# Two transformer blocks on one core: where the norm factor of the up projection is applied, and where expert weights land

## What is computed

```
h = rms_norm(x, g_pre_ffn)
u = causal_depthwise_conv(h @ w_up, conv_w, conv_b)      # 1024 -> 5632, 3 taps
gate, val = split(u)
f = (gelu(gate) * val) @ w_down                           # 2816 -> 1024
x = x + rms_norm(f, g_post_ffn)
e = p @ w_ple                                             # embedding, 256 -> 1024
g = sigmoid(rms_norm(x, g_ple_gate) @ w_ple_gate + b_ple_gate)
x = x + rms_norm(g * e, g_post_ple)
```

## Time and profile before

| | |
|---|---|
| median of three runs | 919.2 us (918.31 to 919.8) |
| the profiled execution, its own time | 917.52 us |
| its span, first to last instruction | 915.6 us |
| granted clock of TensorE, mean | 0.924 |
| PE busy | 769.0 us (84%) |
| DVE / ACT / POOL busy | 383.0 / 328.8 / 128.0 us |
| moved by DMA | 298.48 MB, mean 326 GB/s |

### The profile page before, as it was taken

One profiled execution on the slowest core, in us unless ns is written; L12 is line 12 of the kernel. 1 busy time (PEld: TensorE's weight loads), 2 busy tenths in 40 slices (PEclk: granted clock), 3 DMA queues, 4 the chain that ended last, 5 costly groups with the idle time before them and its releaser, 6 DMA issues.

```text
span 915.6 us, 12692 instructions
## 1 busy us (share of the span) xinstructions
PE 769.0 (84%) x5298; PEld 527.4 (58%) x5298; DVE 383.0 (42%) x838; ACT 328.8 (36%) x656; POOL 128.0 (14%) x130
## 2 busy tenths in 40 slices
PE   9999999999999999999999985668675575655575
PEld 7986579999998867898785431223221222212223
DVE  5757776667779764899613110010100100101002
ACT  5756767666665467824723010001000000000012
POOL 0021042555541033103010000000000000000000
PEclk9999999999999999999999997878778887887877
DMA  9956709755069782646579999999999999999995
GB/s 356 422 193 230 318 1 374 292 185 184 2 278 394 280 337 78 263 175 229 220 306 356 428 447 420 431 434 432 437 433 422 432 437 425 436 432 428 432 421 241
DMA packets 19359, 298.48 MB, mean 326 GB/s; under 512 B 2144, under 2 KB 2528, under 8 KB 5856
## 3 DMA queue, kind: packets, MB, share of 16 engines
q1 hardware_dynamic: 19296, 297.61, 78.7%
HBM read 296.55 MB, written 1.05 MB: 325 GB/s over the span
## 4 chain that ended last, share of the span: by engine, by line
PE 56%; DMA 30%; DVE 9%; ACT 3%; issue 1%; SPq 0%; DVEq 0%; ACTq 0%
PE ps L114 56%; DMA ring<-in_exps 30%; DVE ar L140 3%; DVE fr L132 2%; ACT L120 1%; DVE ar L132 1%; DVE hT L140 0%; ACT sq L120 0%; PE ps L117 0%; ACT ar L123 0%; DVE xg L140 0%; ACT ar L120 0%; ACT yT L120 0%; DVE yT L140 0%; ACT hT L120 0%
## 5 line engine op out<-in xcount | busy, mean ns | idle before, releaser
L114 PE MATMUL ps<-fr 128*128 128x256 f32 (+2 forms) x1308 | 206.7, 314 | 1.1 <-ACT fr L120 0.4
L114 PEld LDWEIGHTS ps<-fr 128*128 128x128 f32 (+1 forms) x1308 | 182.9, 189 | 19.3 <-issue 2.1
L114 PE MATMUL ps<-ring,sq 128*32 128x512 f32 x944 | 129.7, 703 | 74.9 <-DMA ring<-in_exps 74.5
L114 PE MATMUL ps<-ring,ar 128*32 128x512 f32 (+4 forms) x792 | 97.1, 594 | 49.4 <-DMA ring<-in_exps 45.4
L114 PEld LDWEIGHTS ps<-ring,sq 128*32 128x32 f32 x944 | 31.8, 126 | 163.6 <-DMA ring<-in_exps 87.9
L132 DVE TENSOR_TENSOR fr<-ring,fr 128x512 fp32r<-128x512 f32 (+1 forms) x120 | 93.8, 808 | 40.2 <-ACT fr L123 40.1
L132 DVE TENSOR_TENSOR ar<-ar,ps 128x512 f32<-128x512 f32 x9 | 6.2, 687 | 242.3 <-PE ps L114 241.3
L114 PEld LDWEIGHTS ps<-ring,ar 128*32 128x32 f32 (+1 forms) x792 | 29.8, 125 | 101.5 <-issue 50.9
L123 ACT ACTIVATE fr<-ring 128x512 fp32r<-128x512 f32 (+1 forms) x139 | 80.1, 622 | 22.6 <-PE ps L114 20.0
L123 ACT ACTIVATE ar<-ps 128x512 f32<-128x512 f32 (+4 forms) x48 | 27.2, 571 | 153.6 <-PE ps L117 130.7
L132 DVE TENSOR_TENSOR ar<-ps,ar 128x512 f32<-128x512 f32 (+6 forms) x38 | 23.4, 632 | 120.5 <-PE ps L114 120.2
(11 more groups left out here) (193 smaller groups left out, 896.5 us busy)
## 6 DMA issues: line engine op xcount, KB each, us to landing
ring<-in_exps SPq DMA_DIRECT2D x21, 4096.0 KB, 28.4
ring<-in_exps SPq DMA_DIRECT2D x10, 6144.0 KB, 26.9
ring<-in_modw SPq DMA_DIRECT2D x12, 2048.0 KB, 13.8
ring<-in_exps SPq DMA_DIRECT2D x12, 2048.0 KB, 12.6
ring<-in_wup SPq DMA_DIRECT2D x11, 2048.0 KB, 14.0
ring<-in_wdown SPq DMA_DIRECT2D x5, 2048.0 KB, 12.7
ring<-in_exps SPq DMA_DIRECT2D x9, 1024.0 KB, 10.8
ring<-in_win SPq DMA_DIRECT2D x4, 2048.0 KB, 11.2
```

The costliest lines, as they stand in the source:

```text
L114: return Issue(self.e and self.e.matmul(o, l, r, start=start, stop=stop, skip_group_check=True))
```

## The change

Up slabs: x is rounded right after the residual add, times `g_pre_ffn` but without the norm factor. PE starts slab 0 on that; the squares, their sums, the root and the turned factor are made during slabs 0 and 1, and DVE multiplies each finished bank by the factor (`normed`, two instructions a slab, 128x512 in PSUM) ahead of `conv_base` and the taps, which move back by one to two parts. f, f_hi and f_lo move behind part 7, f_hi and f_lo into the next slab behind parts 1 and 0, and `mod_column` from part 1 to part 7. `mod_total(1)` moves ahead into the output projection; the silu of the conditioning row moves into slab 4, and the gelu table is loaded again in slab 5. Six parts of slab 0 have their rests on POOL.

Embedding: p and `w_ple` are rounded during the down stage (five roundings on ACT, five rests on POOL), and `embed` makes three products of rounded parts. The gate's first half uses banks 0 and 7, so that it no longer waits until the embedding has left its banks. In the next stage half a `mod_half` stands where idle products stood.

Routing: `token_major` writes its rows straight into the output banks and leaves them there for the sum, `over_tokens` goes; the last squares are summed by PE, not first by DVE; an expert product waits for its own x tile only.

Expert loads: piece 6 and piece 7 are loaded place by place, with waits of their own; the first half of piece 12 goes into `xT`, and the other halves of 12 to 14 follow half a slot behind.

```diff
-POOL_UP = {("lo", 0, k) for k in (0, 1, 2, 3, 5, 7)} | {("lo", j, k) for j in range(1, 11) for k in (3, 7)}
+POOL_UP = {("lo", 0, k) for k in range(6)} | {("lo", j, k) for j in range(1, 11) for k in (3, 7)}
...
+        def half_place(j, h):
+
+            if (j, h) == (12, 0):
+                return xT
+            i, o = {(12, 1): (0, 0), (13, 0): (0, 2048), (13, 1): (4, 0), (14, 0): (4, 2048), (14, 1): (1, 0)}[j, h]
+            return slot("exps", i)[:, o:o + 2048]
...
             column_sums(5, [(tile(sq, k), act_wo["osq", k // 2]) for k in range(4)]).then_inc(pe_wo, "sums", 1)
+            mod_total(1)
             out_products(range(2), 1, range(1))
...
-            pe.wait_ge(act_wo["root", 1])
-            idle_products(1, 5)
-            token_sums("mix", 2, dve_joint["mix", "mt", 1, 0])
-            idle_products(1, 5)
-            token_columns("mix", 2)
-            idle_products(2, 5)
-            pe.wait_ge(dve_joint["mix", "rrecip"])
-            turned_over(3, misc[:, 118:120]).then_inc(pe_joint, "mix", "over")
-            mod_total(1, act_wo["root", 1])
...
+                    if (j, k) == (0, 7):
+                        column_sums(2, [(tile(sq, i), pool_up["squares", i // 4]) for i in (0, 1, 4, 5)]).then_inc(pe_joint, "mix", "sums")
+                    if (j, k) == (1, 0):
+                        token_columns("mix", 2)
+                    if (j, k) == (1, 1):
+                        pe.wait_ge(dve_joint["mix", "rrecip"])
+                        turned_over(3, misc[:, 118:120]).then_inc(pe_joint, "mix", "over")
...
             def embed(j, n, *free):
-                pe.wait_ge(loaded("wple", 0), landed["p"]["all"], *free)
+                _, ph, pl = p_parts()
+                pe.wait_ge(pool_gate["p_lo"], *free)
                 for k in range(2):
-                    t = pe.matmul(bank(5 + j), ar[:, pT + k * S + 128 * j:pT + k * S + 128 * j + 128],
-                                  slot("wple", 0)[:, k * 1024 + 512 * n:k * 1024 + 512 * n + 512], k == 0, k == 1)
+                    _, wh, wl = ple_parts(2 * k + n)
+                    c = slice(k * S + 128 * j, k * S + 128 * j + 128)
+                    pe.matmul(bank(5 + j), ph[:, c], wh, k == 0, False)
+                    pe.matmul(bank(5 + j), ph[:, c], wl, False, False)
+                    t = pe.matmul(bank(5 + j), pl[:, c], wh, False, k == 1)
                 t.then_inc(pe_gate, "e", j, n)
...
             token_sums("ple", 2, dve_joint["ple", "x", 1])
-            idle_products(1, 5)
+            mod_quarter(11, 1, 0)
             token_columns("ple", 2)
-            mod_half(11, 1)
+            mod_quarter(11, 1, 1)
...
-                return tuple((act_exp if i in (1, 3, 7) else dve_exp)["x", 0, i] for i in (k - k % 2, k - k % 2 + 1))
+                return ((act_exp if k in (1, 3, 7) else dve_exp)["x", 0, k],)
...
-            x_squares("mix")
-            joint_row("mix", 2, 116)
-            for k in range(8):
-                act.wait_ge(dve_up["h", k])
-                act.copy(tile(fr, k, XH), tile(yT, k)).then_inc(act_up, "x_hi", k)
+
+            def up_input(k):
+                act.wait_ge(dve_joint["mix", "x", k])
+                act.copy(tile(fr, k, XH), tile(xT, k), col("g_pre_ffn", k)).then_inc(act_up, "x_hi", k)
+
+            for i in range(4):
+                up_input(2 * i)
+                if i == 3:
+                    up_rounded(0, 6)
+                up_input(2 * i + 1)
+                if i == 3:
+                    up_rounded(0, 7)
+                act.activation(sq[:, i * 512:(i + 1) * 512], xT[:, i * 512:(i + 1) * 512], ACT.Square).then_inc(act_joint, "mix", "xsq", i)
+                if i in (1, 2):
+                    up_rounded(0, 3 + i)
+            up_rounded(1, 0)
+            up_rounded(1, 1)
+            act.wait_ge(pe_joint["mix", "sums"])
+            act.copy(sd[:, 0, :], half(2, 0)).then_inc(act_joint, "mix", "sums")
+            up_rounded(1, 2)
+            act.wait_ge(pe_joint["mix", "cols"])
+            row_root(misc[:, 116:118], ps[:, 2, S:S + 2], 32 * 1024).then_inc(act_joint, "mix", "rroot")
+            act.activation(misc[:, 2:3], eps, ACT.Gelu_apprx_tanh).then_inc(act_up, "tables")
 
 
             def conv_base(j, p):
-                act.wait_ge(pe_up[j, 7], pool_up["f_lo", j - 2] if j > 1 else dve_up["x_lo", 7])
+                act.wait_ge(dve_up["normed", j, p], pool_up["f_lo", j - 2] if j > 1 else None)
                 for i in range(2):
                     f = 2 * j + i + 22 * p
                     act.activation(conv_place(j, p)[:, S * i:S * i + S], half(up_bank(j, p), i), ACT.Identity, scale=col("conv_w", 88 + f),
                                    bias=col("conv_b", f)).then_inc(act_up, "base", j, p, i)
 
             def conv_step(j, step):
-                if step == 1:
+                if step == 3:
                     conv_base(j, 0)
-                elif step == 3:
+                elif step == 4:
                     conv_base(j, 1)
                 elif step == 5:
                     act.wait_ge(dve_up["conv", j, 0])
                     act.activation(conv_place(j, 0), conv_place(j, 0), ACT.Gelu_apprx_tanh).then_inc(act_up, "gelu", j)
-                elif step == 7:
+                elif step == 9:
                     act.wait_ge(pool_up["f", j])
                     act.copy(fr[:, FH + 512 * j:FH + 512 * j + 512], conv_place(j, 0)).then_inc(act_up, "f_hi", j)
 
-            for j in range(11):
-                for k in range(8):
-                    if j or k > 3:
-                        up_rounded(j, k)
-                    if j:
+            for j in range(1, 11):
+                for k in range(3 if j == 1 else 0, 8):
+                    up_rounded(j, k)
+                    if j == 1:
+                        conv_step(0, k - 1)
+                    else:
                         conv_step(j - 1, k)
-                if j == 0:
-                    act.wait_ge(landed["crow"]["all"])
-                    act.activation(sq[:, 0:1024], sq[:, 0:1024], ACT.Silu).then_inc(act_mod, "crow")
+                        if k == 1:
+                            conv_step(j - 2, 9)
+                    if (j, k) == (4, 6):
+                        act.wait_ge(landed["crow"]["all"])
+                        act.activation(sq[:, 0:1024], crow, ACT.Silu).then_inc(act_mod, "crow")
+                    elif (j, k) == (5, 1):
+                        act.activation(misc[:, 2:3], eps, ACT.Gelu_apprx_tanh).then_inc(act_up, "again")
...
-                if i > 1 and i % 2 == 0:
-                    conv_step(10, i // 2)
-                if (f, n) == (8, 1):
+                if i == 1:
+                    conv_step(9, 9)
+                if i in (6, 8, 10, 18):
+                    conv_step(10, {6: 3, 8: 4, 10: 5, 18: 9}[i])
+                if (f, n) == (11, 1):
                     act.activation(misc[:, 2:3], eps, ACT.Sqrt).then_inc(act_down, "tables")
+                if i in (30, 33, 36, 39):
+                    w, hi, _ = ple_parts((i - 30) // 3)
+                    act.wait_ge(loaded("wple", 0))
+                    act.copy(hi, w).then_inc(act_gate, "ple", (i - 30) // 3)
+                if i == 27:
+                    p, hi, _ = p_parts()
+                    act.wait_ge(landed["p"]["all"])
+                    act.copy(hi, p).then_inc(act_gate, "p")
...
+            def input_rest(k):
+                dve.wait_ge(act_up["x_hi", k])
+                dve.scalar_tensor_tensor(tile(fr, k, XL), tile(xT, k), col("g_pre_ffn", k), tile(fr, k, XH).bitcast(F32),
+                                         ALU.mult, ALU.subtract).then_inc(dve_up, "x_lo", k)
+
+            def normed(j, p):
+
+                u = by(bank(up_bank(j, p)), S)
+                dve.wait_ge(pe_up[j, 7], dve_joint["mix", "row"])
+                dve.tensor_tensor(u, u, wide(rb[:, 1, :], 2), ALU.mult).then_inc(dve_up, "normed", j, p)
+
+            def up_rest(j, k):
+                if ("lo", j, k) not in POOL_UP:
+                    hi, lo = weight_place(8 * j + k)
+                    dve.wait_ge(act_up["hi", j, k])
+                    dve.tensor_tensor(lo, slot("wup", j)[:, 512 * k:512 * k + 512], hi.bitcast(F32), ALU.subtract).then_inc(dve_up, "lo", j, k)
+
             for k in range(9):
                 if k < 8:
-                    dve.wait_ge(pe_joint["mix", "over"])
-                    dve.scalar_tensor_tensor(tile(yT, k), tile(xT, k), col("g_pre_ffn", k), half(3, 0), ALU.mult, ALU.mult).then_inc(dve_up, "h", k)
+                    add_turned("mix", k, (6, 7, 0, 1)[k // 2], col("g_post_mix", k))
                 if k:
-                    dve.wait_ge(act_up["x_hi", k - 1])
-                    dve.tensor_tensor(tile(fr, k - 1, XL), tile(yT, k - 1), tile(fr, k - 1, XH).bitcast(F32), ALU.subtract).then_inc(
-                        dve_up, "x_lo", k - 1)
-            mod_total(1)
...
                 for k in range(8):
-                    if ("lo", j, k) not in POOL_UP:
```

(68 more changed lines are left out.)

141 lines of the change are left out of this document (78 added, 63 removed).

## The result

The changed kernel takes 923.45 us (median of six runs, 921.47 to 924.05) against 918.96 for the kernel before: a ratio on record of 1.0046 (not quite the quotient of the two medians), 95% interval 1.0036 to 1.0057, so 0.46% slower. Its profiled execution has a span of 921.5 us, 5.9 more than before. By the medians it is 4.5: the execution that was profiled before took 917.52 us, less than its median, so differences between the two profiles add up to 1.4 too much. The forecast was 921.8 and slower. One execution of the last experiment ran at a mean granted clock of 0.555 and took 1258.69 us, the other four 910.4 to 912.29; without it the median given there, 911.59, would be 911.53.

The account below looks back on a forecast made before the run. TensorE's chain was taken to bound the kernel first, the DMA engines in the experts; terms summed to +2.55 us on the profiled 917.52, giving 920.1, with the median 1.7 above at 921.8. Range 909 to 928, the forecast's own 918 to 927.

Parts of the forecast that it names:

- The start: Start of the up projection: slab 0's products begin 6.8 us sooner; `mod_total` in the output projection gives back 0.7.
- The loop of VectorE: Up slabs: f and f_lo on GpSimd exclude VectorE's rests, so its loop is 11.56 us against PE's 11.45.
- slabs without a column: Slabs 2 to 7: each costs 0 to 0.7 us, taken as 0.4 x 6 = +2.4.
- behind columns: Loops beginning with a column in slabs 8 to 10: 2.2 us over PE's, three times, +6.6; start of down +1.05.
- the silu and the table load: ACT in slabs 4 and 5: silu and second gelu load ahead of roundings cost 0 to 2 us, taken +0.7.
- slabs 0 and 1: First two up slabs: starting without a lead costs 0.5 to 3 us, taken +1.5; sums between products add +1.7.
- Rival A: Up slabs: GpSimd falls into VectorE's waits, PE stays the bound, loop terms go; sum -9.2, 910.0 us; chance 0.22.
- Rival B: Up slabs: only columns bite, 1.3 us in each of three slabs and 0.5 in down; 914.4 us; chance 0.16.
- Embedding and gate: Embedding to gate: rounded products and freed banks save 0.4 to 1.7 us, taken -1.3; the quarter `mod_half` -0.4.
- Routing: Routing to expert products: no VectorE squares, no wait for the second x tile, `over_tokens` gone; -1.2 us.
- The loads: Expert loads: 1 MiB more place in `xT` shortens the dense DMA stream, taken -2.4 us, between -3.8 and +0.6.
- Rival C: Expert loads: the extra MiB gives nothing or loses up to 0.6, the rest as forecast; about 924.5 us; chance 0.17.

Follow-up runs that it names:

- the last experiment: Changed kernel with f and f_lo on VectorE, all squares summed by TensorE and the gelu table loaded two parts later: 911.59 us, 0.9921 of the kernel before.
- short columns: Changed kernel with the four columns of slabs 7 to 10 made over 8 of their 1024 elements: 916.54 us, 0.9974 of the kernel before.
- 1.75 by the experiment: Changed kernel with a plain copy instead of the silu in slab 4 and no second gelu table load: 921.7 us, 1.0035 of the kernel before.
- the first experiment: Changed kernel with f and its rest f_lo moved from GpSimd to VectorE: 913.54 us, 0.9944 of the kernel before.
- the two experiments with f: Changed kernel with f and f_lo on VectorE, 913.54 us; changed kernel with GpSimd's f on 8 of 512 columns, 913.51 us.
- the kernel with halves in the ring: Changed kernel with the six halves of pieces 12 to 14 in ring slots as before, none in xT: 926.29 us, 1.0088 of the kernel before.

## Why the prediction was right

**The start** was right: from the first output products (106.20 before, 107.32 after) to slab 0 it is 34.63 before and 28.38 after, 6.25 less, against 6.8 - 0.7 = 6.1 forecast. The execution was already 1.1 late at the output products; over the profiles of the changed kernel and its variants, all the same up to there, they begin between 106.25 and 107.32, so that part of the difference is scatter.

**The loop of VectorE** was right in its mechanism and nearly in its size. For the terms between slab 0 and the gate I had 1.7 + 1.5 + 2.4 + 6.6 + 1.05 + 0.7 = 13.95, and 141.44 - 127.08 = 14.36 up to down, and 0.96 in down, were measured. Within it:
- slabs without a column: 11.56 was forecast for a loop with f and f_lo in it, and slabs 3, 4 and 6 have 11.6. Slab 2 lasts from 163.25 to 175.87, 12.62, and lost 12.62 - 11.52 = 1.1, so these cost 1.3 together, not 2.4. Slab 2's part went by ACT's wait for f as well, which the sum did not have.
- behind columns: slabs 7 to 10 lost 1.04 and three times 1.88, 6.7, against 7.65 with the start of down. With short columns it is 6.9 less. The upper bound in the sum, 14.6, does not come out of its own terms: 12.77 and a rest of 1.30 are 14.07. The middle of 12.77 and 14.07 is 13.42, and 13.40 was measured.
- the silu and the table load: 0.7 was taken and 13.71 - 11.52 = 2.2 measured, 1.75 by the experiment. The sum counted the silu and one table load. ACT's lines have two loads, 1.28 us each, at 193.13 and 199.82, with a silu of 1.06, and between them the wait of 2.12 for f. ACT has time for the silu and the loads alone (the first experiment), but not with that wait, and VectorE's loop had no room left to catch up with late roundings. This term was mis-sized most.
- slabs 0 and 1: from 135.70 to 163.25 it is 27.55, two slabs are 23.04, the three groups of sums 0.64 + 0.50 + 0.38 = 1.5, so the stalls are 3.0, the upper bound; 1.5 was taken.

Rival A, that GpSimd falls into VectorE's waits, is refuted by the two experiments with f; with f out of the way they land at 913.5, 3.5 above A's 910.0. Rival B, columns alone, took 4.4 us for them where 6.7 were lost, and lacks slabs 2 and 5. Two bounds of the prediction do not follow from its words: two thirds more of the loop terms (10.75) would make the forecast's upper end 929, not 927, and the sum of all low ends leaves out what it calls the least for the columns, 3.9 + 0.5, so it would be 912.6, not 908.2. The measured time lies inside either way.

The rule of the Trainium skill, page "SBUF — State Buffer", section "SBUF: two separate sides", holds in every pair of lines above (2.31 for 1.21, 1.78 for 0.68) in that one of the two runs and the other waits, and taps and `normed`, with one input in PSUM, kept their 0.41 and 0.64 throughout.

**Embedding and gate**: -1.3 forecast, -1.26 measured (11.52 from the first embedding product to the gate before, 10.26 after). The quarter product: -0.4 and -0.36 (8.93 at the gate, 8.57 at the next stage). That the five roundings cost nothing held in the four profiles in which their loads had landed. Where ACT waited for the loads, down was 0.4 to 0.96 longer, 0.96 here: through the loads, not through ACT's time.

**Routing** was the wrong step: -1.2 forecast, +0.25 measured up to the first expert product (8.57 late ahead of the stage, 8.83 behind it). Of the 0.25, 0.22 is a wait ahead of the routing (0.53 at 435.63, 0.31 before), which is 0.29 to 0.53 in the experiments. At the last but one group of logits (489.69, and 480.88 before) the kernel is 8.81 late, so the routing itself gained nothing and lost nothing. The wait for the second x tile (0.33) did go. What came in its place:

```profile
490.05 1.14 PE L114 MATMUL ps<-con,xg 128*128 128x128 f32 x8
...
491.84 0.58 PE L114 MATMUL ps<-con,sq 128*128 128x1 f32 x4
...
496.16 0.43 PE L114 MATMUL ps<-ar,misc 128*128 128x64 f32 x2 [0.51 <-DVE ar L136]
```

What I did not count is that the first `token_major`, which took 0.63 before, now takes 1.14, and that the first pair of sums stands ahead of the last logits. So the last sums begin at 491.84 where they began at 482.60 before, 9.24 later, 0.4 more than the stage; VectorE's choice of the experts is that much later, and TensorE waits 0.51 for it. This is read from the timelines; no run undoes it alone. The 1.9 us that `over_tokens` freed behind the first expert product lie where the end is set by DMA: the kernel with halves in the ring has that gain too and the same 425.9 as before.

**The loads**: -2.4 forecast, -2.84 to -3.3 measured by the experiment, -2.9 in the pair of profiles. Rival C, which had 923.5 for that experiment, is refuted.

The sum of what was measured, 1.1 - 6.25 + 14.36 + 0.96 - 1.26 - 0.36 + 0.25 - 2.9, is 5.9, the difference of the spans. Its errors are the silu (+1.5), the stalls of slabs 0 and 1 (+1.5), routing (+1.45), down (+0.96), the scatter ahead (+1.1) and, the other way, the other slabs (1.3 + 6.7 - 2.4 - 7.65 = -2.05), the loads (-0.5) and small ones (-0.6). The scatter and the wait in down vary from execution to execution. The others cancel in part: the mechanism and the sign were foreseen, but that the median came within 1.7 us of the forecast, with single terms off by 1.5, is partly luck.

## What to carry to other kernels

Add up, for the engine that feeds the bottleneck, the loop from one hand-over to the next, and put into it not only its own instructions but also those of an engine that excludes it: here four GpSimd instructions of 1.3 us or more took (1.58 - 0.68) + (2.31 - 1.21) + (2.37 - 1.36) + (1.78 - 0.68) = 4.1 us out of one loop of VectorE although VectorE's busy share before, 26.88 of 34.00, left room. Look, too, at what an engine in the middle waits for: ACT held its roundings back for f. Two instructions that cost half on the busier engine and nothing in exclusion were cheaper there; its busy time even fell, from 32.37 to 31.58 us of the window 214 to 248, since time spent waiting for GpSimd counts as busy. A fault in one stage can hide gains in others: the change as a whole lost 4.5 us, while its other parts alone gain 4.0, and all of it with f moved gains 5.4 and with the better start 6.9, each against the kernel before of its group.

## What the runs showed that I had not expected

A GpSimd instruction does not always get its turn between two VectorE instructions, as I took from the earlier trace rows. With f on VectorE, a GpSimd rest that takes 1.30 alone stood for 3.17 us (3.60 and 3.63 behind the next two columns):

```profile
227.57 3.17 POOL L132 TENSOR_TENSOR fr_h<-ring,fr_h 128x512 fp32r<-128x512 f32 x1 [4.46 <-ACT fr_h L123]
```

VectorE's lines beside it stand in the first experiment: f and the column began after it (0.69 and 1.22, neither longer than alone), and the GpSimd instruction got in only behind the column, inside the two rests that took 2.38. "The one that asked first" of the prediction is thus not borne out here. What decides which engine goes first was not tried.

And a column over 8 elements was not short. In that experiment, VectorE and GpSimd:

```profile
232.38 1.25 DVE L162 CUSTOM_DVE_ANT_0 sq<-ring,sq 128x8 f32<-128x8 f32 x1
```

```profile
231.99 1.62 POOL L132 TENSOR_TENSOR yT<-yT 128x512 f32<-128x512 f32 x1
```

The column stands for 1.25 us, about as long as the full one of 1.21, and ends at 233.63, as f does on GpSimd (233.61). In the changed kernel it is 2.31 and ends 1.1 behind f: wait and work one after the other. Over 8 elements next to nothing but the wait is left. A VectorE line that is longer than its work is thus how such an exclusion looks; it does not look like idle time.
